# State-space scan: the 16 rotation tables made during the first projection tiles, kept in DRAM and loaded step by step

## The chip, the core and the metric
One core of a Trainium2 chip runs the whole kernel in one launch. The metric is the device time of that launch in microseconds (us); lower is better.

## The reference, cut to what matters
The kernel computes one block of a network on 512 tokens of width 2048: an RMS norm, a wide input projection, a state-space branch, an mLSTM branch, a gated merge, and a layer of experts. The change touches the state-space branch only.

```
proj = hn @ w_in          # split into u_ssm (512), xm (1536), z (1536), i, f, g_a (2048), g_b (2048)
a_bar  = exp(lam * dt)                                   # one complex number for each of 2048 states
bu     = einsum('gph,bsgh->bsgp', b_bar, u)              # complex input of every state, 512 tokens
states = scan over tokens: s[t] = a_bar * s[t-1] + bu[t]
y      = real(einsum('ghp,bsgp->bsgh', c, states)) + d_skip * u ; y = gelu(y)
```

The 2048 states are 16 blocks of 128 partitions. With a_bar = r * exp(i*theta), the kernel turns bu[t] back by the angle theta*t, runs two real scans with the factor r, and turns the result forward again. For this each block of states needs a table of cos(theta*t) and sin(theta*t), 128 x 512 each. That is a rotation table. The sixteen tables depend on the parameters alone, not on the tokens.

## The kernel before
**Engines and order.** The order on every engine is written out by hand, with semaphores. PE is TensorE, DVE is VectorE, ACT is ScalarE, POOL is GpSimd. SP issues the weight stream: one unit is a 128 x 2048 tile of weights (1024 KB) that lands in `raw[k]`, k = 0 or 1.

**One unit of the stream.** Products are made in fp32 as three matmuls of split operands. ACT copies `raw` to `whi` (line 653, in `split_hi`), DVE makes `wlo = raw - whi` (line 1038, in `split_lo`, called by `next_lo`), and PE does 48 matmuls of 512 columns (`proj`, lines 1732 to 1734). `split_hi` of unit u+1 waits until PE is done with unit u-1, since that frees `whi[k]` (the condition in `next_hi`, line 657). ACT then stores PE's result to DRAM (`spilled`, lines 688 to 695). So each unit passes ACT, DVE and PE in this order, and PE starts unit u+1 once `lo_done` has counted its `wlo`.

**The first projections.** Units 4 to 15 give xm and units 16 to 27 give z. DVE's part is two loops of `next_lo`: lines 1204 to 1206 (it makes `wlo` of units 5 to 16) and lines 1214 to 1216 (units 17 to 26). Between the two loops stand three small instructions on the gates (lines 1211 to 1213). The third counts `ge_sem` to 1, and ACT waits for that with an exponential (lines 701 and 702) that stands ahead of its `split_hi` of unit 17. Behind the second loop stands the gate section of DVE (lines 1218 to 1235). Its last instruction counts `ge_sem` to 3, and ACT waits for that at line 707, ahead of its `split_hi` of unit 27. DVE then makes `wlo` of units 27 and 28 (lines 1236 and 1237).

**The scan.** Units 28 to 59 (the gates g_a, g_b) share their stretch with the scan: 4 chunks c of 4 steps k (lines 1240 to 1291 on DVE, 1789 to 1806 on PE, 375 to 408 on POOL, 713 to 729 on ACT). A step of PE is: projection unit, the output matmuls of the step before (`s5_out`, lines 1784 and 1786), the two input products into `sc` (line 1804), a second projection unit. At the end of a chunk PE does `s5_out` of step 3 at once, so it waits for that step's `rout`. A step of DVE is: `wlo`; the rotation table of this block (lines 1249 to 1263: two memsets, then nine levels that each double the table with four instructions, 38 instructions in all); the rotation of the inputs (1267 to 1269), once ACT has copied `sc` to `bus` (line 723); two scans (1274, 1276); `wlo` of the next unit; the rotation back into `rout` (1280 to 1283). POOL does half of each rotation (lines 391 to 405). In a level, the second and the fourth instruction start without a wait; the others wait for the one before them.

**Addresses.** The cosines and sines of theta*2^lv of all 16 blocks are in `ptab`. POOL copies the four blocks of a chunk into the small tile `pc` (lines 382 and 383), and the level loop takes its two scalars as `pc[:, 0, lv, k:k + 1]` and `pc[:, 1, lv, k:k + 1]` (line 1253), whose addresses are constants. The only other place that matters here is the short convolution `conv` (lines 1294 to 1307): its scalars `tap` are addressed by `3 * h + c`. Called at line 1312, h is the constant 0; called from `head` (lines 1395, 1398 and 1404) inside the loop over heads, h is a loop register. 

`tab` has two buffers, so the table of step k may be written once the outputs of step k-2 are done.

Of the kernel before, what the change touches and what calls it, by code (L numbers as in the profile page):

```python
# [13 lines left out]
ALU = mybir.AluOpType  # L14
ACT = mybir.ActivationFunctionType
AX_X = mybir.AxisListType.X
F32 = mybir.dt.float32
# [4 lines left out]
P = 128  # L22
T = 512
# [3 lines left out]
SC, MC, HC = SSM_W // P, ML_W // P, HD // P  # L27
# [7 lines left out]
U_SSM, U_XM, U_Z, U_GA, U_GB = 0, 4, 16, 28, 44  # L35
# [28 lines left out]
HALF_PI = (1.5703125, 4.837512969970703125e-4, 7.54978995489188216e-8)  # L64
NEG_BIG = -3.0e38

S5_STEPS, ML_STEPS, PK_STEPS, PICK_STEPS = 164, 23, 67, 64


def build(nc, a, out_d):  # L70

    ctx = ExitStack()
    with ctx:
# [3 lines left out]
        def S(name, shape, dt, kb):  # L77

            size = 4 * int(np.prod(shape[1:]))
            assert kb * 1024 + size <= room, (name, kb * 1024 + size, room)  # L80
            return nc.alloc_sbuf_tensor_at(name, shape, dt, offset=base + int(kb * 1024))

        def sem(name):
            return ctx.enter_context(nc.semaphore(name))
# [28 lines left out]
        wif = S("wif", [P, KC, 64], F32, 164)  # L113
        bc = S("bc", [P, 2, P], F32, 168)
        cc = S("cc", [P, 2, 4, 32], F32, 169)
        pc = S("pc", [P, 2, 9, 4], F32, 170)
        rc = S("rc", [P, 8], F32, 170.5)
        cw = S("cw", [P, 40, 16], F32, 171)
        ptab = S("ptab", [P, 2, 9, 16], F32, 174)
        gt = S("gt", [P, 4, T], F32, 184)  # L120
        gout = S("gout", [P, 3, T], F32, 192)
        tab = S("tab", [P, 2, 2, T], F32, 112)
# [4 lines left out]
        dtmp = S("dtmp", [P, 2, T], F32, 136)  # L127
# [99 lines left out]


        spill = nc.dram_tensor("spill", (56, P, T), F32).ap()
        ya_d = nc.dram_tensor("ya_d", (KC, P, T), F32).ap()  # L230
        ev_d = nc.dram_tensor("ev_d", (NKEY * NKEY, D), F32).ap()
        gates_d = nc.dram_tensor("gates_d", (3, HEADS, T), F32).ap()
# [47 lines left out]
        idx_done, el_in, ac_done, acc_done = sem("idx_done"), sem("el_in"), sem("ac_done"), sem("acc_done")  # L280
        gv_in = [sem(f"gv_in{i}") for i in range(3)]
        acct_done, acct_free = sem("acct_done"), sem("acct_free")
        gn_in, upn_in = sem("gn_in"), [sem("upn_in0"), sem("upn_in1")]
        ev_out = sem("ev_out")
        fin_done, fin_out = sem("fin_done"), sem("fin_out")
# [52 lines left out]
        def _(pool):  # L338
            n = [0]
# [26 lines left out]
                                   ALU.subtract).then_inc(alo_done[1], 1)  # L366


            pool.wait_ge(gates_done, 1)
            pool.dma_start(gates_d.rearrange("g h t -> h g t"), gout[0:HEADS, :, :]).then_inc(gates_out, 16)  # L370


            pool.wait_ge(coef_done, 1)
            pool.wait_ge(proj_free, SC)
            with pool.Fori(0, SC) as c:

                pool.wait_ge(cm_done, 4 * c)
                pool.wait_ge(ylo_done, c)
                pool.tensor_copy(uc[:], uT[:, c, :])
                for r in range(2):  # L380
                    pool.tensor_copy(cc[:, r, :, :], cp[:, r, :, :].rearrange("p (c k) h -> p c k h", c=4)[:, c, :, :])
                    pool.tensor_copy(pc[:, r, :, :],
                                     ptab[:, r, :, :].rearrange("p n (c k) -> p c n k", c=4)[:, c, :, :])
                pool.tensor_copy(rc[:, 0:4], cw[:, 0, :].rearrange("p (c k) -> p c k", c=4)[:, c, :])
                pool.tensor_copy(rc[:, 4:5], vec[:, V_DSKIP:V_DSKIP + SC].rearrange("p (c k) -> p c k", k=1)[:, c, :])\
                    .then_inc(chunk_done, 1)
                for k in range(4):

                    pool.wait_ge(bus_done, 8 * c + 2 * k + 2)
                    pool.wait_ge(tab_done, 4 * c + k + 1)  # L390
                    pool.tensor_tensor(ptmp[:, 0, :], bus[:, 1, :], tab[:, k % 2, 0, :], ALU.mult).then_inc(pool_step, 1)
                    pool.tensor_tensor(ptmp[:, 1, :], bus[:, 0, :], tab[:, k % 2, 1, :], ALU.mult).then_inc(pool_step, 1)
                    pool.wait_ge(pool_step, 2 + 16 * c + 4 * k + 2)

                    pool.wait_ge(scan_done, 8 * c + 2 * k)
                    pool.tensor_tensor(rin[:, 1, :], ptmp[:, 0, :], ptmp[:, 1, :], ALU.subtract).then_inc(prot_done, 1)

                    pool.wait_ge(prot_done, 4 * c + k + 1)
                    pool.wait_ge(scan_done, 8 * c + 2 * k + 2)
                    pool.tensor_tensor(ptmp[:, 0, :], wst[:, 0, :], tab[:, k % 2, 1, :], ALU.mult).then_inc(pool_step, 1)  # L400
                    pool.tensor_tensor(ptmp[:, 1, :], wst[:, 1, :], tab[:, k % 2, 0, :], ALU.mult).then_inc(pool_step, 1)
                    pool.wait_ge(pool_step, 2 + 16 * c + 4 * k + 4)

                    pool.wait_ge(cm_done, 4 * c + k)
                    pool.tensor_tensor(rout[:, 1, :], ptmp[:, 0, :], ptmp[:, 1, :], ALU.add).then_inc(out_i_done, 1)

                pool.wait_ge(bu_done, 8 * c + 8)
                pool.dma_start(bc[:], a["b_tab"][c + 1]).then_inc(bc_in, 16)
# [598 lines left out]
        def _(dve):  # L1007
# [33 lines left out]
            def next_lo(m, k):  # L1041
                nm, nk = (m, 1) if k == 0 else (m + 1, 0)
                split_lo(nm, nk)
# [157 lines left out]
            tt(cp[:, 1, :, :], w0, cp[:, 1, :, :], ALU.add)  # L1201
            dve.tensor_scalar(cp[:, 1, :, :], cp[:, 1, :, :], -1.0, None, ALU.mult).then_inc(coef_done, 1)

            with dve.Fori(U_XM // 2, U_Z // 2) as m:
                for k in range(2):
                    next_lo(m, k)


            gi, g1, g2, gf = (gt[0:HEADS, i, :] for i in range(4))
# [1 line left out]
            ts(gi, pv[0][0:HEADS, :], vec[0:HEADS, V_BI:V_BI + 1], None, ALU.add)  # L1211
            ts(gf, pv[0][32:32 + HEADS, :], vec[32:32 + HEADS, V_BF:V_BF + 1], None, ALU.add)
            dve.scalar_tensor_tensor(g1, gf, -1.0, gf, ALU.mult, ALU.max).then_inc(ge_sem, 1)
            with dve.Fori(U_Z // 2, U_GA // 2 - 1) as m:
                for k in range(2):
                    next_lo(m, k)

            dve.wait_ge(ge_sem, 2)
            ts(g1, g2, 2.0, None, ALU.add)
# [18 lines left out]


            with dve.Fori(0, SC) as c:  # L1240
                one, count = stepper(s5_step, S5_STEPS * c)
                dve.wait_ge(chunk_done, c + 1)
                for k in range(4):
                    m = U_GA // 2 + 4 * c + k
                    next_lo(m, 0)

                    dve.wait_ge(out_i_done, 4 * c + k - 1 if k else 4 * c)
                    tc_, ts_ = tab[:, k % 2, 0, :], tab[:, k % 2, 1, :]
                    one(dve.memset(tc_[:, 0:1], 1.0), wait=False)
                    one(dve.memset(ts_[:, 0:1], 0.0))  # L1250
                    for lv in range(9):
                        w = 1 << lv
                        pcos, psin = pc[:, 0, lv, k:k + 1], pc[:, 1, lv, k:k + 1]
                        one(dve.tensor_scalar(dtmp[:, 0, 0:w], ts_[:, 0:w], psin, None, ALU.mult), wait=False)
                        one(dve.tensor_scalar(dtmp[:, 1, 0:w], ts_[:, 0:w], pcos, None, ALU.mult))
                        one(dve.scalar_tensor_tensor(tc_[:, w:2 * w], tc_[:, 0:w], pcos, dtmp[:, 0, 0:w],
                                                     ALU.mult, ALU.subtract), wait=False)
                        ins = dve.scalar_tensor_tensor(ts_[:, w:2 * w], tc_[:, 0:w], psin, dtmp[:, 1, 0:w],  # L1258
                                                       ALU.mult, ALU.add)
                        if lv < 8:  # L1260
                            one(ins)
                        else:
                            ins.then_inc(tab_done, 1)
                    dve.wait_ge(tab_done, 4 * c + k + 1)

                    dve.wait_ge(bus_done, 8 * c + 2 * k + 2)
                    one(dve.tensor_tensor(dtmp[:, 0, :], bus[:, 0, :], tc_, ALU.mult), wait=False)
                    one(dve.tensor_tensor(dtmp[:, 1, :], bus[:, 1, :], ts_, ALU.mult))
# [884 lines left out]
```

## Time and profile before

| what | value |
|---|---|
| time, median of 3 runs | 4286.54 us (4284.75 to 4287.95) |
| time of the profiled execution | 4285.1 us |
| its span, first to last instruction | 4283.6 us |
| PE busy | 4065.0 us (95%) |
| DVE busy | 2508.7 us (59%) |
| ACT busy | 1226.7 us (29%) |
| POOL busy | 1129.3 us (26%) |
| mean granted clock of PE | 0.973 of full speed |

The span is the profiled execution without what lies around it, here 1.5 us. Busy times count only instructions that work on data; matmuls overlap and their ends are modelled. In a timeline a row gives the start and the time of an instruction, and in brackets how long the engine had been idle before it and what released it. A row marked DVEq is work of DVE's sequencer (register arithmetic), not of its data path. A window row gives the busy time and the number of instructions of each engine, then the granted clock of PE (1.00 is 2.4 GHz, 0.5 is 1.2 GHz), the DMA share and the rate.

### The profile page before, as it was taken

To read this page: it belongs to the slowest core of one execution; us is meant where nothing else is said; L and a number is where in the kernel's file an instruction comes from. 1 tells how busy PE (TensorE), PEld (TensorE's weight loads), DVE (VectorE), ACT (ScalarE), POOL (GpSimd) and SP (SyncE) were. 2 spreads that over 40 slices of the span, in tenths; PEclk is the share of its full clock that TensorE was granted. 3 is DMA by queue.
4 is the path that set the end of the run, shared out by engine and by line. 5 is a ranking of instruction groups with operands and counts; after the bars stand their busy time and mean duration, and the time that the engine had idled before them with its cause. 6 is when DMAs were issued, how large, how long until landed. Compare 5 with 4: busy or idle time off the path is not lost.

```text
span 4283.6 us, 54780 instructions
## 1 busy us (share of the span) xinstructions
PE 4065.0 (95%) x19189; PEld 3474.4 (81%) x19189; DVE 2508.7 (59%) x3563; ACT 1226.7 (29%) x1282; POOL 1129.3 (26%) x742
## 2 busy tenths in 40 slices
PE   7999999887789989999999999999989999999997
PEld 4887666665677768888888888888879999999996
DVE  5226888837653254454566666222237888788874
ACT  3232222234322222222233333222222222232222
POOL 1002334433211144545300000000012444444432
PEclk9999999998899989999999999999999999999998
DMA  3332222342154344554677777866767888888883
GB/s 120 120 115 98 98 100 96 108 152 79 51 175 142 127 135 162 173 170 161 209 238 239 255 241 238 295 216 215 222 232 262 302 306 325 308 327 304 307 315 114
DMA packets 225639, 840.57 MB, mean 196 GB/s; under 512 B 21720, under 2 KB 60136, under 8 KB 157600
## 3 DMA queue, kind: packets, MB, share of 16 engines
q1 hardware_dynamic: 96432, 454.07, 29.3%
q10 hardware_dynamic: 95808, 207.64, 15.6%
q0 software_dynamic: 33328, 178.08, 11.5%
q8 instruction: 25, 0.41, 0.0%
q14 instruction: 46, 0.38, 0.0%
HBM read 753.70 MB, written 220.23 MB: 227 GB/s over the span
## 4 chain that ended last, share of the span: by engine, by line
PE 72%; DVE 13%; issue 6%; DMA 4%; ACT 3%; POOL 2%; DVEq 1%; ACTq 0%; SPq 0%; POOLq 0%
PE mm L1732 18%; PE mm L1733 18%; PE mm L1734 17%; DMA raw<-stream 3%; PE pv L1732 3%; PE pv L1733 3%; PE pv L1734 3%; DVE wlo L1038 2%; PE sc L1734 1%; PE sc L1733 1%; PE sc L1732 1%; DVE acc L1658 1%; ACT whi L653 1%; DVE tab L1258 1%; POOL el L611 1%
## 5 line engine op out<-in xcount | busy, mean ns | idle before, releaser
L1038 DVE TENSOR_TENSOR wlo<-raw,whi 128x2048 fp32r<-128x2048 f32 x328 | 753.4, 2297 | 882.4 <-ACT whi L653 881.9
L653 ACT ACTIVATE whi<-raw 128x2048 fp32r<-128x2048 f32 x380 | 727.4, 1914 | 499.6 <-issue 198.7
L1732 PE MATMUL mm<-t_hi,whi 128*128 128x512 f32 x2048 | 798.5, 390 | 0.0
L1733 PE MATMUL mm<-t_lo,whi 128*128 128x512 f32 x2048 | 797.8, 390 | 0.0
L1734 PE MATMUL mm<-t_hi,wlo 128*128 128x512 f32 x2048 | 797.3, 389 | 0.0
L1734 PEld LDWEIGHTS mm<-t_hi,wlo 128*128 128x128 f32 x2048 | 384.6, 188 | 80.4
L1732 PEld LDWEIGHTS mm<-t_hi,whi 128*128 128x128 f32 x2048 | 384.8, 188 | 78.1
L1733 PEld LDWEIGHTS mm<-t_lo,whi 128*128 128x128 f32 x2048 | 384.8, 188 | 77.7
L1732 PE MATMUL mm<-hn_hi,whi 128*128 128x512 f32 x960 | 380.6, 396 | 34.3 <-DVE hn_lo L1074 19.3
L1733 PE MATMUL mm<-hn_lo,whi 128*128 128x512 f32 x960 | 376.6, 392 | 0.0
L1734 PE MATMUL mm<-hn_hi,wlo 128*128 128x512 f32 x960 | 375.9, 392 | 0.0
L617 POOL DMA_INDIRECT gv<-ev_d,idx_v x128 | 230.1, 1798 | 513.7 <-DVE acc L1658 468.7
L550 POOL TENSOR_TENSOR wlo<-raw,whi 128x2048 fp32r<-128x2048 f32 x52 | 239.3, 4603 | 301.0 <-ACT whi L653 301.0
L1658 DVE SCALAR_TENSOR_TENSOR acc<-gv,ac,acc 128x2048 f32<-128x2048 f32 x127 | 298.2, 2348 | 32.5 <-DMA gv<-ev_d,idx_v 30.3
L894 ACT ACTIVATE sgl<-mm 128x512 f32<-128x512 f32 x128 | 76.7, 599 | 744.9 <-PE mm L1734 744.8
L1732 PEld LDWEIGHTS mm<-hn_hi,whi 128*128 128x128 f32 x960 | 181.7, 189 | 95.6 <-issue 33.8
L611 POOL DMA_INDIRECT el<-up_d,idx_e x128 | 198.2, 1548 | 88.0 <-DVE ac L1664 49.2
L1734 PEld LDWEIGHTS mm<-hn_hi,wlo 128*128 128x128 f32 x960 | 181.9, 189 | 38.5
L1733 PEld LDWEIGHTS mm<-hn_lo,whi 128*128 128x128 f32 x960 | 182.0, 190 | 36.5
L961 ACT ACTIVATE actb<-gl 128x384 f32 (+1 forms) x128 | 67.3, 526 | 492.5 <-DVE gl L1633 484.6
L1732 PE MATMUL pv<-actb,whi 128*128 (+1 forms) x512 | 173.0, 338 | 13.7 <-DVE wlo L1038 13.7
L1732 PE MATMUL mm<-actb,whi 128*128 (+1 forms) x512 | 171.7, 335 | 0.4 <-DVE wlo L1038 0.3
(395 smaller groups left out, 7553.1 us busy)
## 6 DMA issues: line engine op xcount, KB each, us to landing
raw<-stream SPq DMA_DIRECT2D x380, 1024.0 KB, 4.9
ev_d<-stream ACTq DMA_DIRECT2D x128, 1024.0 KB, 6.1
up_d<-sgl ACTq DMA_DIRECT2D x128, 256.0 KB, 2.1
g_d<-gst ACTq DMA_DIRECT2D x12, 2048.0 KB, 11.5
gg<-g_d SPq DMA_DIRECT2D x15, 1536.0 KB, 12.0
gl<-up_d SPq DMA_DIRECT2D x120, 192.0 KB, 5.0
spill<-stage ACTq DMA_DIRECT2D x56, 256.0 KB, 2.0
x<-xT SPq DMA_DIRECT2D x4, 1024.0 KB, 9.4
```

What stands on the lines that cost most here:

```text
L550: pool.tensor_tensor(wlo[:, nk, :], raw[:, nk, :], whi[:, nk, :].bitcast(F32), ALU.subtract)\
L611: pool.indirect_dma_start(el[:, s:s + 1], None, ups_flat, bass.IndirectOffsetOnAxis(ap=idx_e[:, s:s + 1], axis=0)).then_inc(el_in, 16)
L617: pool.indirect_dma_start(gv[s % 3][:], None, ev_d, bass.IndirectOffsetOnAxis(ap=idx_v[:, 0, s:s + 1], axis=0))\
L653: act.activation(whi[:, k, :], raw[:, k, :], ACT.Copy).then_inc(hi_done, 1)
L894: act.activation(sgl[:, k, :], mm[k][:], ACT.Gelu_apprx_tanh).then_inc(proj_free, 1)
L961: act.activation(actb[:, par, 0, v, :], gl[:, v % 2, :], ACT.Copy).then_inc(acthi_done, 1)
L1038: dve.tensor_tensor(wlo[:, k, :], raw[:, k, :], whi[:, k, :].bitcast(F32), ALU.subtract)\
L1258: ins = dve.scalar_tensor_tensor(ts_[:, w:2 * w], tc_[:, 0:w], psin, dtmp[:, 1, 0:w], ALU.mult, ALU.add)
L1658: dve.scalar_tensor_tensor(acc[:], gv[b][:], ac_cols[:, s, :], acc[:], ALU.mult, ALU.add)\
L1732: pe.matmul(out, lh, rh, start=start, stop=False)
L1733: pe.matmul(out, lh, rl, start=False, stop=False)
L1734: return pe.matmul(out, ll, rh, start=False, stop=stop)
```

## The change
The table of a block is no longer made in its step of the scan. DVE makes all sixteen during the projections: in the first loop one table behind every two units (6 tables), in the second loop one behind every unit (10 tables). POOL stores each table in a DRAM tensor `tab_d` when `tab_done` has counted it, and DVE waits for the store of two tables before it overwrites a buffer. In the scan POOL loads the table of a step, 512 KB, one step ahead (`table`), and DVE and POOL wait for the load (`tab_in`) where they waited for the table. The copies into `pc` are gone; the level loop takes its scalars from `ptab` at the place n, which is an expression of the loop register.

```
+        tab_d = nc.dram_tensor("tab_d", (4 * SC, P, 2, T), F32).ap()
@@ POOL
+            with pool.Fori(0, 2 * SC) as q:
+                for b in range(2):
+                    pool.wait_ge(tab_done, 2 * q + b + 1)
+                    pool.dma_start(tab_d[2 * q + b], tab[:, b, :, :]).then_inc(tab_out[b], 16)
             pool.wait_ge(gates_done, 1)
...
+            def table(n, k, half):
+                pool.wait_ge(tab_out[k % 2], 16 * 2 * SC)
+                pool.wait_ge(out_r_done, n - 1 if k else n)
+                pool.wait_ge(out_i_done, n - 1 if k else n)
+                pool.dma_start(tab[:, k % 2, :, :], tab_d[n]).then_inc(tab_in[k % 2], 16)
             with pool.Fori(0, SC) as c:
+                table(4 * c, 0, 2 * c)
...
-                    pool.tensor_copy(pc[:, r, :, :],
-                                     ptab[:, r, :, :].rearrange("p n (c k) -> p c n k", c=4)[:, c, :, :])
...
                 for k in range(4):
+                    if k < 3:
+                        table(4 * c + k + 1, k + 1, 0)
                     pool.wait_ge(bus_done, 8 * c + 2 * k + 2)
-                    pool.wait_ge(tab_done, 4 * c + k + 1)
+                    pool.wait_ge(tab_in[k % 2], 32 * c + 16 * (k // 2) + 16)
@@ DVE
-            with dve.Fori(U_XM // 2, U_Z // 2) as m:
-                for k in range(2):
-                    next_lo(m, k)
+            def rotation_table(n, b, half):
+                one, count = stepper(s5_step, TAB_STEPS * n)
+                dve.wait_ge(tab_out[b], 16 * half)
+                tc_, ts_ = tab[:, b, 0, :], tab[:, b, 1, :]
+                one(dve.memset(tc_[:, 0:1], 1.0), wait=False)
+                one(dve.memset(ts_[:, 0:1], 0.0))
+                for lv in range(9):
+                    w = 1 << lv
+                    pcos, psin = (ptab[:, r, lv, :].rearrange("p (q o) -> p q o", o=1)[:, n, :] for r in range(2))
+                    one(dve.tensor_scalar(dtmp[:, 0, 0:w], ts_[:, 0:w], psin, None, ALU.mult), wait=False)
+                    one(dve.tensor_scalar(dtmp[:, 1, 0:w], ts_[:, 0:w], pcos, None, ALU.mult))
+                    one(dve.scalar_tensor_tensor(tc_[:, w:2 * w], tc_[:, 0:w], pcos, dtmp[:, 0, 0:w],
+                                                 ALU.mult, ALU.subtract), wait=False)
+                    ins = dve.scalar_tensor_tensor(ts_[:, w:2 * w], tc_[:, 0:w], psin, dtmp[:, 1, 0:w],
+                                                   ALU.mult, ALU.add)
+                    if lv < 8:
+                        one(ins)
+                    else:
+                        ins.then_inc(tab_done, 1)
+            with dve.Fori(0, MC // 4) as j:
+                for b in range(2):
+                    for k in range(2):
+                        next_lo(U_XM // 2 + 2 * j + b, k)
+                    rotation_table(2 * j + b, b, j)
...
-            with dve.Fori(U_Z // 2, U_GA // 2 - 1) as m:
-                for k in range(2):
-                    next_lo(m, k)
+            with dve.Fori(0, U_GA // 2 - 1 - U_Z // 2) as j:
+                for k in range(2):
+                    next_lo(U_Z // 2 + j, k)
+                    rotation_table(MC // 2 + 2 * j + k, k, MC // 4 + j)
...
             with dve.Fori(0, SC) as c:
                 for k in range(4):
                     next_lo(m, 0)
-                    dve.wait_ge(out_i_done, 4 * c + k - 1 if k else 4 * c)
...
-                        pcos, psin = pc[:, 0, lv, k:k + 1], pc[:, 1, lv, k:k + 1]
...
-                    dve.wait_ge(tab_done, 4 * c + k + 1)
+                    dve.wait_ge(tab_in[k % 2], 32 * c + 16 * (k // 2) + 16)
                     dve.wait_ge(bus_done, 8 * c + 2 * k + 2)
```

## Rows read from the trace of the kernel before

**Rows 1.** Busy time by window, one of the z projections and one middle step of the scan
```profile
205.00:333.00 128.00, 128.00 (x566) 106.04 (x565) 29.59 (x15) 41.35 (x33) 0.00 (x0) 1.00 0.33 118
...
412.00:438.00 26.00, 26.00 (x106) 18.95 (x105) 24.71 (x50) 6.40 (x7) 11.14 (x6) 1.00 0.31 102
```

**Rows 2.** Timeline of PE: the input products of two steps that follow each other
```profile
413.33 1.98 PE L1804 MATMUL sc<-uc,bc 32*128 32x512 f32 x4
...
439.08 1.98 PE L1804 MATMUL sc<-uc,bc 32*128 32x512 f32 x4
```

**Rows 3.** Waits of PE in the scan (366 to 825 us): total us, times, longest us
```profile
PE dn L1784 <- DVE rout L1283: 18.3, 4, 4.7
PE mm L1732 <- DVE wlo L1038: 6.9, 4, 2.5
```

**Rows 4.** Timeline of DVE: the end of the xm projections, z projections, gate section
```profile
228.29 2.29 DVE L1038 TENSOR_TENSOR wlo<-raw,whi 128x2048 fp32r<-128x2048 f32 x1 [8.45 <-ACT whi L653]
230.50 1.51 DVE L1099 TENSOR_SCALAR gt<-pv,vec 4x512 f32<-4x512 f32 x2
...
240.94 2.29 DVE L1038 TENSOR_TENSOR wlo<-raw,whi 128x2048 fp32r<-128x2048 f32 x1 [8.22 <-ACT whi L653]
...
338.29 2.29 DVE L1038 TENSOR_TENSOR wlo<-raw,whi 128x2048 fp32r<-128x2048 f32 x1 [8.43 <-ACT whi L653]
340.50 0.41 DVE L1099 TENSOR_SCALAR gt<-gt 4x512 f32<-4x512 f32 x1
...
359.89 2.29 DVE L1038 TENSOR_TENSOR wlo<-raw,whi 128x2048 fp32r<-128x2048 f32 x1 [2.49 <-ACT whi L653]
```

**Rows 5.** Timeline of PE: the first matmul of unit 27
```profile
362.23 0.79 PE L1732 MATMUL mm<-hn_hi,whi 128*128 128x512 f32 x1 [6.82 <-DVE wlo L1038]
```

**Rows 6.** Timeline of DVE: the rotation table of step 1, chunk 0
```profile
407.53 0.06 DVE L1249 MEMSET tab<- 128x1 f32 x1
...
407.66 0.21 DVE L1254 TENSOR_SCALAR dtmp<-tab,pc 128x1 f32<-128x1 f32 x1
407.79 0.20 DVE L1255 TENSOR_SCALAR dtmp<-tab,pc 128x1 f32<-128x1 f32 x1
...
415.67 0.48 DVE L1258 SCALAR_TENSOR_TENSOR tab<-tab,pc,dtmp 128x256 f32<-128x256 f32 x1
```

**Rows 7.** Convolution on DVE: constant address, then a loop register; last the register instructions
```profile
831.76 0.54 DVE L1300 TENSOR_SCALAR cv<-xmr,vec 128x512 f32<-128x512 f32 x1
832.34 1.54 DVE L1302 SCALAR_TENSOR_TENSOR cv<-xmr,vec,cv 128x511 f32<-128x511 f32 x2
...
1002.36 0.75 DVE L1302 SCALAR_TENSOR_TENSOR cv<-xmr,vec,cv 128x511 f32<-128x511 f32 x1 [0.15 <-DVE cv L1300]
...
L1302 DVEq FUSED_REGOPS  x18: 57/57/65, 988.4 to 1065.6; - x18
```

**Rows 8.** Timeline of ACT: the exponential between the xm and the z projections
```profile
237.05 0.63 ACT L702 ACTIVATE gt<-gt 4x512 f32<-4x512 f32 x1 [0.68 <-ACT stage L693]
```

**Rows 9.** Timelines of ACT and DVE: `bus` and the rotation behind it, two steps
```profile
466.49 1.09 ACT L723 ACTIVATE bus<-sc 128x512 f32<-128x512 f32 x2 [2.74 <-PE sc L1804]
...
467.80 1.80 DVE L1267 TENSOR_TENSOR dtmp<-bus,tab 128x512 f32<-128x512 f32 x1
...
612.04 1.09 ACT L723 ACTIVATE bus<-sc 128x512 f32<-128x512 f32 x2 [0.70 <-ACT stage L693]
...
614.96 1.78 DVE L1267 TENSOR_TENSOR dtmp<-bus,tab 128x512 f32<-128x512 f32 x1
```

**Rows 10.** Timeline of DVE: the first rotation product in step 1 of chunk 2
```profile
642.00 0.69 DVE L1267 TENSOR_TENSOR dtmp<-bus,tab 128x512 f32<-128x512 f32 x1 [1.47 <-ACT bus L723]
```

**Rows 11.** Timeline of PE behind its longest wait for `wlo`; busy time by window
```profile
624.83 0.64 PE L1732 MATMUL mm<-hn_hi,whi 128*128 128x512 f32 x1 [2.46 <-DVE wlo L1038]
...
625.00:635.50 10.50, 10.50 (x40) 8.53 (x41) 10.11 (x24) 0.53 (x1) 4.13 (x3) 0.84 0.52 169
```

**Rows 12.** DMA issues on POOL's queue: KB each, median us to landing
```profile
sz<-spill POOLq DMA_DIRECT2D x4, 768.0 KB, 7.0
```

More of the change, by code:

```diff
@@ L65 @@
 NEG_BIG = -3.0e38
-S5_STEPS, ML_STEPS, PK_STEPS, PICK_STEPS = 164, 23, 67, 64
+S5_STEPS, TAB_STEPS, ML_STEPS, PK_STEPS, PICK_STEPS = 16, 37, 23, 67, 64
 def build(nc, a, out_d):
@@ L115, in build @@
         cc = S("cc", [P, 2, 4, 32], F32, 169)
-        pc = S("pc", [P, 2, 9, 4], F32, 170)
         rc = S("rc", [P, 8], F32, 170.5)
@@ L282, in build @@
         acct_done, acct_free = sem("acct_done"), sem("acct_free")
+        tab_out, tab_in = [sem("tab_out0"), sem("tab_out1")], [sem("tab_in0"), sem("tab_in1")]
         gn_in, upn_in = sem("gn_in"), [sem("upn_in0"), sem("upn_in1")]
@@ L1202, in _ @@
             dve.tensor_scalar(cp[:, 1, :, :], cp[:, 1, :, :], -1.0, None, ALU.mult).then_inc(coef_done, 1)
-            with dve.Fori(U_XM // 2, U_Z // 2) as m:
-                for k in range(2):
-                    next_lo(m, k)
+            def rotation_table(n, b, half):
[17 more added lines that the diff above has]
+                        ins.then_inc(tab_done, 1)
+                assert count[0] == TAB_STEPS, count
+            with dve.Fori(0, MC // 4) as j:
[3 more added lines that the diff above has]
+                    rotation_table(2 * j + b, b, j)
             gi, g1, g2, gf = (gt[0:HEADS, i, :] for i in range(4))
@@ L1240, in _ @@
             with dve.Fori(0, SC) as c:
-                one, count = stepper(s5_step, S5_STEPS * c)
+                one, count = stepper(s5_step, TAB_STEPS * 4 * SC + S5_STEPS * c)
                 dve.wait_ge(chunk_done, c + 1)
@@ L1245, in _ @@
                     next_lo(m, 0)
-                    dve.wait_ge(out_i_done, 4 * c + k - 1 if k else 4 * c)
                     tc_, ts_ = tab[:, k % 2, 0, :], tab[:, k % 2, 1, :]
[L1249 to L1252, printed above, removed]
-                        pcos, psin = pc[:, 0, lv, k:k + 1], pc[:, 1, lv, k:k + 1]
[L1254 to L1263, printed above, removed]
-                    dve.wait_ge(tab_done, 4 * c + k + 1)
+                    dve.wait_ge(tab_in[k % 2], 32 * c + 16 * (k // 2) + 16)
                     dve.wait_ge(bus_done, 8 * c + 2 * k + 2)
```

## The prediction
> **What bounds the kernel now.** I first read the busy time by window. In the z projections PE is busy for all of the 128 us, with 566 matmuls, 0.226 us each, so a unit of 48 takes 10.86 us; DVE works 29.59 us of the 128 [rows 1]. There PE is the bound and DVE has room. In a middle step of the scan both are full: PE 26.00 of 26 us, DVE 24.71 [rows 1]. The question is which of the two sets the step. The timeline of PE answers it: from one pair of input products to the next it is 25.75 us [rows 2], and the list of PE's waits has only eight entries in the whole scan [rows 3]: four for `rout` at the chunk ends (18.3 us together) and four for `wlo` (6.9 us), one in step 0 of each chunk. The twelve other steps have no wait of PE. So in the scan PE is the bound too, DVE is the bound for 25.2 us in all, and that is the most that freeing DVE can return, apart from the clock.
>
> The place to look at next is where the work goes. The timeline of DVE shows the ten `wlo` of the z projections (first and last shown), then the gate section from 340.50 us on, and `wlo` of unit 27 at 359.89 [rows 4]. PE stood idle for 6.82 us before that unit [rows 5]. So the chain DVE gate section, ACT, DVE `wlo`, PE is already late there: whatever delays the start of the gate section delays PE one for one, however idle DVE was on the way.
>
> **What leaves the scan.** A table takes from 407.53 to 415.67 + 0.48 = 416.15, that is 8.62 us [rows 6]; 16 of them are 138 us of DVE. Most of that lies under PE's units. The gain is how much earlier the rotation starts. It needs the table and `bus`; where the table is in time, DVE waits for `bus` alone [rows 10]. In step 0 of chunk 2 `bus` is done at 613.13 and the rotation starts at 614.96, 1.8 us late [rows 9]; the same step is 0.8, 0.7 and 0.9 us late in the other chunks. The `wlo` behind it comes earlier by that, 4.1 us for the four. The wait of 2.46 us in chunk 2 is also followed by a stretch at 0.84 granted clock, a part of it at the lower level, 1.2 GHz [rows 11]; with 0.8 us of wait left, as long as the waits that stayed at full clock or shorter, I count 0.16 x 10.5 = 1.7 us back. In step 3 the rotation starts 0.2 us late [rows 9], up to 0.3 in the other chunks: 1 us for the four chunk ends. A rotation that starts with DVE ahead of POOL has a first product of 0.69 us where it otherwise takes 1.8 [rows 9, 10]; I count a few tenths for that. The sum is **7 us gained**, with 3 and 12 as the ends. The copies into `pc` are off every path, since the `wlo` behind them waits for ACT: nothing.
>
> **What comes to the projections: the tables.** Their instructions are the same, but the scalars are now addressed by a loop register. The convolution has both forms. With constant addresses the next instruction starts 0.04 us behind the end of the last (831.76 + 0.54, then 832.34); with a loop register it is 0.15, and DVE's sequencer shows one register instruction of 57 ns for each [rows 7]. A table has 18 instructions that wait for the one before, so it grows by 18 x 0.11 = 2.0 us. The other 18 follow at 0.13 us (407.66 to 407.79 us in the smallest level) and no row shows a register instruction inside such a pair: bounds are nothing, if it fits into the 0.13, and 57 ns each, 1.0 us. I take the middle: the table is 8.6 + 2.0 + 0.5 = **11.1 us**, ends 10.6 and 11.6. A `wlo` ahead of it takes 2.21 us until the next instruction starts (228.29 to 230.50) [rows 4]. In the second loop DVE then needs 13.3 us a unit against PE's 10.86.
>
> The Trainium skill speaks against this term: "VectorE: DVE Perf Modes", section "The DRAIN you can't avoid", says that the next instruction starts only when the pipe is empty and that a semaphore between two costs nothing extra. If register work hid in the same way the table would stay at 8.6 us. The convolution's 0.15 against 0.04 us is the measurement, and it decides for my sum.
>
> **What comes to the projections: the path.** In the first loop a table stands behind every two units, 2 x 2.21 + 11.1 = 15.5 us of 21.7: it fits. The `wlo` behind a table finds 8.45 us of idle time [rows 4] filled with 11.1, so it is 2.7 us late. PE has more in hand: `wlo` of unit 16 was ready at 230.58 [rows 4] and PE came to it at about 235.8 (ACT's copy of PE's result, 0.6 us, and 0.68 idle lie ahead of the exponential at 237.05 [rows 8]). The sixth table starts at 230.50, where the gate instructions start now; those took until 240.94 - 8.22 = 232.72, 2.22 us [rows 4]. They now end at 230.50 + 11.1 + 2.22 = 243.8. ACT's exponential waits for them and started at 237.05 [rows 8]; `wlo` of unit 17 came 3.89 us behind it (240.94) [rows 4, 8]. Now it comes at 243.8 + 3.9 = 247.7. From there DVE does ten times `wlo` and table, without a pause since it is the slower one: 247.7 + 10 x 13.31 = 380.8 is the new start of the gate section, against 340.50 [rows 4]. In general it is 258.7 + 11 x table. So the chain is **40.3 us later**; with tables of 10.6 and 11.6 us, 34.8 and 45.8. Even with tables of 8.62 it is 13.0. All that follows, the gate section, ACT, `wlo`, unit 27 at 362.23 [rows 5], and the scan behind, moves by this. PE's waits between units are about 2.4 us each, near the 2.46 that was followed by the lower clock [rows 11]; units of 12.6 us still fit into 13.3, so that costs nothing more. PE's idle time before unit 27 becomes some 22 us; it restarts at 1.2 GHz in the kernel before too (first matmuls of 0.79 and 0.64 us behind both waits [rows 5, 11]), so I add nothing.
>
> **The DMAs and the new waits.** POOL issues a store behind each table. It has nothing else there, and DVE overwrites a buffer two tables later, 13 us at least. In the scan a load is issued when the step before has its outputs, about 8 us before the next `bus`. A load of 512 KB lies between nothing and the 7.0 us of 768 KB on the same queue [rows 12]; I take it as hidden. Behind POOL's wait for `rout` is only its own next rotation, which needs the later `bus`. Cost nothing; if the cover were gone, up to 1 us a step.
>
> **Sum.** 4285.1 us (the profiled execution: span 4283.6 and 1.5 around it) + 40.3 - 7 = 4318.4. The median lies 1.4 above that execution, so I say **4320 us**.
>
> **Rivals.**
> - *Register work is hidden.* The table stays at 8.6 us. For it: in the scan each wait of the table has a threshold that is computed in a register, and the table of 8.62 us [rows 6] holds all of them. Against: the convolution's rows [rows 7]. Then 13.0 - 7 = 6: 4293 us. Chance 0.09. It is also what the skill's rule above would give.
> - *Register work costs more.* Each of the 36 instructions pays 0.11 us, since a register instruction breaks the pair too: table 12.6 us, chain 57 us later, 4336 us. Nothing shows it, but no row excludes it. Chance 0.13.
> - *Faster.* DVE sets PE's waits in the scan, as its 24.71 of 26 us suggest [rows 1], and with the tables gone all 25.2 us of waits [rows 3] and 1.7 of clock go. It decides only if the tables cost no register time: 13.0 - 26.9 = -13.9, 4273 us. Against: a chunk end's wait comes from the rotations and scans themselves, which take a unit of 10.86 and up to 4.7 of wait [rows 1, 3], with the table or without. Chance 0.03.
> - *The work doesn't leave the path.* Loads arrive late and each step waits as it did for a table: the gain of 7 is gone, 4327 us. Chance 0.03.
>
> **How the numbers follow.** The forecast, tables of 10.6 to 11.6 us and a gain of 3 to 12, has 0.72 and its own range is 4309 to 4330; its rarer ends and a register cost of two thirds give 4304. About 0.2% (8.6 us) is what a measurement of this kernel can tell from no change. The range of 8 in 10 is 4304 to 4336: it leaves out the hidden register work, the faster case and half of the dearer case. Slower by over 0.2% is the forecast, the dearer tables and the late loads, 0.88 (to 4295 us counts as the same); the first rival lies just inside, 0.09; faster 0.03.
>
> **What would show it.** In the changed kernel: the first instructions of the table pairs with 0.15 us ahead of them and one register instruction of 57 ns for each pointer; a table of some 11 us; ten `wlo` in the z projections with no idle time of DVE ahead of them, 13.3 us apart; `wlo` of unit 17 near 247.8 us; the gate section starting near 381; PE idle some 22 us before unit 27; in the scan, waits of PE for `wlo` of 0 to 1 us and unchanged steps of 25.75. It would be wrong if the gate section starts before 370 (tables cheaper), or if PE's waits at the chunk ends shrink by more than 1 us each.

## The result and the profile after

The changed kernel takes 4301.47 us, the median of 8 runs (4299.31 to 4305.13), against 4285.61 us for the kernel before (8 runs): 15.9 us more, ratio 1.0037, 95% interval 1.0027 to 1.0047. I had forecast 4320 us, with a range from 4304. The direction was right and the time lies outside the range.

| | before | after | forecast |
|---|---|---|---|
| profiled execution, span, us | 4283.6 | 4301.1 | |
| one table, us | 8.62 (in the scan) | 9.64 | 11.1 |
| gate section starts at, us | 340.50 | 364.88 | 380.8 |
| PE starts unit 27 at, us | 362.23 | 387.23 | about 402.5 |
| last matmul of the last chunk, `dn`, starts at, us | 822.36 | 839.84 | |
| gain in the scan, us | | 7.5 | 7 |

Down the last two rows: unit 27 is 25.0 us late, the last `dn` matmul is 17.5 us late, so the scan gave back 7.5 us, and the span is 17.5 us longer. So behind the scan nothing was gained or lost.

**A table.** The timeline of DVE in the xm projections: the table behind `wlo` of unit 16, its memset, first two levels, last instruction, and what follows it.

```profile
230.21 0.06 DVE L1224 MEMSET tab<- 128x1 f32 x1
...
230.46 0.21 DVE L1229 TENSOR_SCALAR dtmp<-tab,ptab 128x1 f32<-128x1 f32 x1 [0.18 <-DVE tab L1225]
230.59 0.21 DVE L1230 TENSOR_SCALAR dtmp<-tab,ptab 128x1 f32<-128x1 f32 x1
230.84 0.22 DVE L1231 SCALAR_TENSOR_TENSOR tab<-tab,ptab,dtmp 128x1 f32<-128x1 f32 x1
230.97 0.21 DVE L1233 SCALAR_TENSOR_TENSOR tab<-tab,ptab,dtmp 128x1 f32<-128x1 f32 x1
231.33 0.23 DVE L1229 TENSOR_SCALAR dtmp<-tab,ptab 128x2 f32<-128x2 f32 x1
...
239.37 0.48 DVE L1233 SCALAR_TENSOR_TENSOR tab<-tab,ptab,dtmp 128x256 f32<-128x256 f32 x1
239.76 1.51 DVE L1114 TENSOR_SCALAR gt<-pv,vec 4x512 f32<-4x512 f32 x2
```

The view of a single line also counts the instructions of DVE's sequencer (DVEq). The first and the second line of a level have one of them each time; the third, L1231, has none, and its row shows DVE alone. The same holds for the fourth, L1233.

```profile
L1229 DVEq FUSED_REGOPS  x144: 57/57/64, 121.9 to 363.3; - x144
...
L1230 DVEq FUSED_REGOPS  x144: 53/57/57, 122.0 to 363.5; - x144
...
L1231 DVE SCALAR_TENSOR_TENSOR tab<-tab,ptab,dtmp x144: 218/235/486, 122.4 to 364.1; 128x1 f32<-128x1 f32 x16, 128x2 f32<-128x2 f32 x16, 128x4 f32<-128x4 f32 x16, 128x8 f32<-128x8 f32 x16
```

Read the gaps. Before the first instruction of a level it is 0.15 us (230.97 + 0.21 = 231.18, then 231.33), as the convolution had shown [rows 7]. Before the third it is 0.04 (230.59 + 0.21, then 230.84), the gap of a constant address. L1229 makes the register for `psin`, L1230 the one for `pcos`, and L1231 and L1233 use those again. The register instruction of L1230 has no price either: L1230 starts 0.13 us behind L1229, just as in the kernel before [rows 6]. So 9 of the 18 waiting instructions pay 0.11 us, not 18, and the in-pair ones nothing: 8.62 + 9 x 0.11 = 9.6, and 9.64 was measured (230.21 to 239.85, the end of L1233).

**The chain.** The timeline of DVE again, its `wlo` of units 17, 18, 25 and 26, the start of the gate section, and `wlo` of unit 27.

```profile
245.92 2.29 DVE L1053 TENSOR_TENSOR wlo<-raw,whi 128x2048 fp32r<-128x2048 f32 x1 [3.93 <-ACT whi L668]
...
257.99 2.28 DVE L1053 TENSOR_TENSOR wlo<-raw,whi 128x2048 fp32r<-128x2048 f32 x1
...
341.19 2.29 DVE L1053 TENSOR_TENSOR wlo<-raw,whi 128x2048 fp32r<-128x2048 f32 x1
...
352.99 2.28 DVE L1053 TENSOR_TENSOR wlo<-raw,whi 128x2048 fp32r<-128x2048 f32 x1
...
364.88 0.41 DVE L1114 TENSOR_SCALAR gt<-gt 4x512 f32<-4x512 f32 x1
...
384.27 2.91 DVE L1053 TENSOR_TENSOR wlo<-raw,whi 128x2048 fp32r<-128x2048 f32 x1 [2.49 <-ACT whi L668]
```

From unit 18 to unit 26 no `wlo` has idle time ahead of it, where each had 8.2 to 8.4 us [rows 4]. They stand 11.9 us apart against the 10.86 of a unit on PE. The prediction's formula, 258.7 + 11 x table, gives 364.7 for the measured table; the gate section starts at 364.88, 24.4 us late. Unit 27 is 25.0 us late on PE, 0.6 more, since its `wlo` takes 2.91 us where it took 2.29 [rows 4]. It takes 2.9 us in the six kernels in which POOL issues a load of a table just ahead of its copy into `uc` (after, e1, e2, e4, e6 and e7), so that this copy of 0.62 us falls inside `wlo`, and 2.29 in the four in which it doesn't (before, e3, e3b and e5). No run tried whether the copy is the cause. PE pays for the delay at unit 27, with the same half-speed start as before [rows 5] but three times the idle time. The longer wait has no clear price of its own in clock: over the 11 us behind this start the granted clock is 0.85 before and 0.78 after, but 0.72 in e4 with 7.4 us of idle time and 0.85 in e5 with 20.

```profile
387.23 0.80 PE L1755 MATMUL mm<-hn_hi,whi 128*128 128x512 f32 x1 [20.64 <-DVE wlo L1053]
```

**The scan.** The waits of PE from 385 to 850 us, in the columns of [rows 3].

```profile
PE mm L1755 <- DVE wlo L1053: 22.9, 5, 20.6
PE dn L1807 <- DVE rout L1306: 17.2, 4, 4.3
```

Of the 22.9 us, 20.6 are the one before unit 27; the other four, in the first steps, are 2.3 us together, where they were 6.9. The chunk ends wait 17.2 us instead of 18.3. That is 4.6 + 1.1 = 5.7 us of the 7.5. The wait in chunk 2 is now short enough that the clock stays up behind it: 1.00 in the window below, against 0.84 [rows 11], the 1.7 us that the forecast had. Elsewhere in the scan the clock falls a little more than before, by 0.7 us, if windows of 11 us are summed from unit 27 on (12.0 us lost to the clock before, 11.0 after). So some 0.8 us of the 7.5 are not accounted for. By window (columns: PE, PE weight load, DVE, ACT and POOL busy, granted clock, DMA share, GB/s):

```profile
645.00:656.00 11.00, 10.44 (x46) 8.50 (x46) 7.89 (x5) 2.52 (x2) 5.69 (x4) 1.00 0.62 192
```

Two middle steps in the same columns, and behind them the input products that mark a step on PE:

```profile
438.00:464.00 26.00, 26.00 (x106) 19.13 (x106) 16.81 (x10) 6.12 (x6) 12.19 (x7) 1.00 0.36 128
464.00:490.00 26.00, 26.00 (x105) 19.09 (x106) 16.84 (x10) 6.12 (x6) 11.55 (x6) 1.00 0.32 105
```

```profile
438.11 1.98 PE L1827 MATMUL sc<-uc,bc 32*128 32x512 f32 x4
...
463.83 1.55 PE L1827 MATMUL sc<-uc,bc 32*128 32x512 f32 x3
```

DVE works 16.8 us of 26 instead of 24.71 [rows 1], a third less, and a step takes 463.83 - 438.11 = 25.72 us instead of 25.75 [rows 2]. PE was the bound of the scan, as read. The DMA issues say that the new transfers are far from late: a load lands 3.6 us behind its issue (median), and each of the 16 first rotation products waits for `bus`, none for a table.

```profile
tab<-tab_d POOLq DMA_DIRECT2D x16, 512.0 KB, 3.6
...
415.41 0.69 DVE L1290 TENSOR_TENSOR dtmp<-bus,tab 128x512 f32<-128x512 f32 x1 [7.89 <-ACT bus L738]
```

### The profile page after: what moved, and what is told of

The parts are those of the page before. It is cut to its first block, busy times and chain, and to the rows that moved or that the text cites. A ratio compares the mean times of both kernels' runs of the same rounds, so it can differ in the third digit from the quotient of the medians.

```text
span 4301.1 us, 55215 instructions
## 1 busy us (share of the span) xinstructions
PE 4066.4 (95%) x19189; PEld 3473.8 (81%) x19189; DVE 2507.5 (58%) x3563; ACT 1226.9 (29%) x1282; POOL 1148.0 (27%) x766
## 4 chain that ended last, share of the span: by engine, by line
PE 79%; DVE 10%; issue 4%; DMA 2%; ACT 2%; POOL 2%; DVEq 1%; ACTq 0%; SPq 0%; POOLq 0%
PE mm L1755 19%; PE mm L1756 19%; PE mm L1757 18%; PE pv L1755 3%; PE pv L1757 3%; PE pv L1756 3%; DVE wlo L1053 2%; DMA raw<-stream 2%; PE sc L1756 2%; PE sc L1757 2%; PE sc L1755 2%; ACT whi L668 1%; PE st L1757 1%; PE dn L1756 1%; PE st L1756 1%
## 5 line engine op out<-in xcount | busy, mean ns | idle before, releaser
L1755 PE MATMUL pv<-actb,whi 128*128 (+1 forms) x512 | 173.3, 339 | 14.8 <-DVE wlo L1053 14.7
L1756 PE MATMUL pv<-actb,whi 128*128 (+1 forms) x512 | 172.2, 336 | 0.0
```

The lines of the kernel that those rows point to most:

```text
L1755: pe.matmul(out, lh, rh, start=start, stop=False)
L1756: pe.matmul(out, lh, rl, start=False, stop=False)
```

## The experiments

**Theory**: the time is set by the start of the gate section, that is by 11 tables in a row on DVE, of 9.64 us each because 9 waiting instructions a table make a register pointer; the scan gains 7.5 us, nearly all in the first steps. **Rivals**: the register pointers cost nothing and the tables are long for another reason; the time comes from the amount of work, stores or loads wherever they stand; the scan gains or loses something that the projections hide. The kernels were run in two sets, each with its own runs of the kernel before: 4282.81 us (21 runs) for the first four, 4282.55 us (27 runs) for the others. Against those, the ratio of 1.0037 puts the changed kernel at 4298.7 and at 4298.4 us.

**e1_constant: the register pointers taken away.** Both loops of DVE are written out, so that every pointer is a constant.

```
-            with dve.Fori(0, MC // 4) as j:
+            for j in range(MC // 4):
...
-            with dve.Fori(0, U_GA // 2 - 1 - U_Z // 2) as j:
+            for j in range(U_GA // 2 - 1 - U_Z // 2):
```

> The two projection loops of DVE are unrolled, so the scalars of the tables have constant addresses; nothing else differs from the changed kernel. Chain theory (the table's own length counts eleven times, gate section at 258.7 + 11 x table): the table falls from 9.64 us to 8.6, the gate section starts at about 353 us instead of 364.9, and the time is 4301.5 - 11 = 4290 us. Rival (the loss comes from the stores and loads, or from the amount of DVE work, not from addressing): table and time stay, 4301 us. Rival 2 (unrolled code costs DVE instruction fetching): table 9 us or more with gaps inside, 4295 to 4301 us.

Measured: 4289.07 us (11 runs), ratio 1.0012 [1.0003, 1.0021]. The last `wlo` of the z projections, the first big gate instruction (L1260, at 365.32 us in the changed kernel), and the start of a table:

```profile
231.51 0.21 DVE L1229 TENSOR_SCALAR dtmp<-tab,ptab 128x1 f32<-128x1 f32 x1
231.65 0.21 DVE L1230 TENSOR_SCALAR dtmp<-tab,ptab 128x1 f32<-128x1 f32 x1
...
343.13 2.28 DVE L1053 TENSOR_TENSOR wlo<-raw,whi 128x2048 fp32r<-128x2048 f32 x1
...
354.34 3.34 DVE L1260 RECIPROCAL gt<-gt 4x512 f32<-4x512 f32 x1
```

The gate section is 10.98 us earlier than in the changed kernel, 1.0 us for each of 11 tables, and the step inside the pair is 0.14 us with a constant and 0.13 with a register. So the pointers cost 1.0 us a table and none of it in the pair. A table takes 8.63 us here, which leaves nothing for the other rival of this run, that written-out code is slower. The kernel is still slower than before: tables of 8.6 us leave a chain that is late, as the prediction's 13.0 us for this case said.

**e2_pointer_each: a register pointer for every instruction.** A second copy of the angle table, read by the third and fourth instruction of each level, so that L1231's pointers can't be those of L1229 and L1230.

```
+                    pcos_b, psin_b = (ptab_b[:, r, lv, :].rearrange("p (q o) -> p q o", o=1)[:, n, :] for r in range(2))
...
-                    one(dve.scalar_tensor_tensor(tc_[:, w:2 * w], tc_[:, 0:w], pcos, dtmp[:, 0, 0:w],
+                    one(dve.scalar_tensor_tensor(tc_[:, w:2 * w], tc_[:, 0:w], pcos_b, dtmp[:, 0, 0:w],
```

> The third and fourth instruction of each level read a second copy of the angle table at another address, so they need a register instruction of their own: nine more waits with a register instruction behind them for each table, which is what my prediction had assumed. Theory: each costs some 0.09 to 0.11 us, the table is 10.5 us, the gate section starts near 374 us and the time is 4301.5 + 9 to 11 = 4311 us. Rival (register work hides and the 0.11 us has another cause, such as the loop or the tile): 4301 us.

Measured: 4307.93 us (5 runs), ratio 1.0054 [1.0040, 1.0068], 9.3 us above the changed kernel on the same scale.

```profile
231.59 0.21 DVE L1233 TENSOR_SCALAR dtmp<-tab,ptab 128x1 f32<-128x1 f32 x1
231.93 0.22 DVE L1234 SCALAR_TENSOR_TENSOR tab<-tab,ptab_b,dtmp 128x1 f32<-128x1 f32 x1
...
374.97 3.34 DVE L1263 RECIPROCAL gt<-gt 4x512 f32<-4x512 f32 x1
```

```profile
L1234 DVEq ALU_OP  x144: 40/40/40, 123.4 to 373.6; - x144
```

The third instruction now has 0.13 us ahead of it instead of 0.04. Its register instruction is another one, ALU_OP of 40 ns and not FUSED_REGOPS of 57, and it costs 0.09 us where the other costs 0.11. A table takes 10.44 us here (231.22 to 241.66), 0.80 more, which is 9 x 0.09. The gate section is 9.65 us later, 0.88 us a table. That is close to the lower end of the prediction, 10.6 us: all 18 waits pay and the pairs nothing. With e1 this brackets the changed kernel from both sides: the price is in the waiting instructions that make a pointer, and their count is what I had wrong.

**e5_proj_alone: the half in the projections.** All 16 tables are made and stored there, as in the changed kernel; the scan is that of the kernel before and makes its own tables again, with no loads, once all stores are done. Against the kernel before, besides the function `rotation_table`, its two calls and the stores:

```
-                    pool.wait_ge(tab_done, 4 * c + k + 1)
+                    pool.wait_ge(tab_done, 16 + 4 * c + k + 1)
...
-                one, count = stepper(s5_step, S5_STEPS * c)
+                one, count = stepper(s5_step, TAB_STEPS * 4 * SC + S5_STEPS * c)
```

> The projections are those of the changed kernel, with all sixteen tables made and stored, and the scan is that of the kernel before, which makes each table again and loads none. Theory: the gate section starts 24.4 us late and the scan gains nothing: 4285.6 + 24.5 = 4310 us. Rival (part of the delay is made good later, since work that waits in the scan is shifted too): 4300 to 4306 us.

**e4_scan_alone: the half in the scan.** Two tables are made early, with constant addresses, and stored eight times each; the scan loads as in the changed kernel. It leaves out the 14 other tables. Against the changed kernel:

```
-                    rotation_table(2 * j + b, b, j)
+                    if j == 0:
+                        rotation_table(b, b, 0)
...
-                    next_lo(U_Z // 2 + j, k)
-                    rotation_table(MC // 2 + 2 * j + k, k, MC // 4 + j)
+                    next_lo(m, k)
```

> Only two tables are made, behind the first two pairs of xm units, and each is stored eight times; the z loop is that of the kernel before. The scan loads one table a step as the changed kernel does. Left out: the other fourteen tables. Theory: the gate section starts at 340.5 as before and the scan keeps its gain of 7.5 us: 4285.6 - 7.5 = 4278 us. Rival (the loads cost something in the scan that the gain hides, or the gain comes from another place): 4283 to 4286 us.

Measured: e5 4307.57 us (5 runs), 1.0059 [1.0045, 1.0072], that is 24.8 us slower; e4 4275.3 us (11 runs), 0.9984 [0.9975, 0.9993], 7.5 us faster. Together 17.3 us slower, and the change is 15.9: the two halves add up. The waits of PE from 300 to 850 us, of e5 and then of e4:

```profile
PE mm L1765 <- DVE wlo L1044: 27.8, 7, 20.1
PE dn L1817 <- DVE rout L1316: 18.3, 4, 4.7
```

```profile
PE dn L1807 <- DVE rout L1306: 17.2, 4, 4.3
PE mm L1755 <- DVE wlo L1053: 9.7, 5, 7.4
```

In e5 the chunk ends wait 18.3 us, as before; in e4 17.2 us, as after, and 7.4 of its 9.7 us are the old wait ahead of unit 27 (6.8 us before; the rest is the longer `wlo`). From the first matmul of unit 27 to the last `dn` matmul it is 460.1 us before, 452.6 after, 452.5 in e4 and 459.7 in e5: the gain in the scan is there with the loads and gone without them. e5 came out at 4307.57 us, between its theory (4310) and its rival (4306 at most); a part of the delay that is made good later is at most 0.4 us by this measure.

**e3_two_late: only the place of two tables.** Tables 14 and 15 are made behind the gate section, where DVE waited 14.37 us for `whi` before `wlo` of unit 29. **e3b_two_late_const** does the same with both loops written out.

```
-            with dve.Fori(0, U_GA // 2 - 1 - U_Z // 2) as j:
+            with dve.Fori(0, U_GA // 2 - 2 - U_Z // 2) as j:
...
+            for k in range(2):
+                next_lo(U_GA // 2 - 2, k)
...
             for k in range(2):
                 next_lo(U_GA // 2 - 1, k)
+            for k in range(2):
+                rotation_table(14 + k, k, 7)
```

> The changed kernel, but its last two tables (14 and 15) are made behind the gate section and the two wlo that follow it, where DVE was idle for 14.4 us before wlo of unit 29; the tables stay loop-addressed, their number, stores and loads are the same. Theory (only the start of the gate section counts): it starts some 15 us earlier, near 349.5 us instead of 364.9, and the kernel takes about 4286 us, 1.001 times the kernel before. Rival (the time is the amount of DVE work, stores or loads, wherever it stands): no change, 4301 us. If the two tables in their new place delay wlo of unit 29 past PE, some 5 us of the 15 are given back: 4291.

> As the kernel with two late tables, but with both loops written out, so that every pointer is a constant address and a table takes 8.57 us instead of 9.64. Theory: DVE keeps up with PE in the z projections, the gate section starts within 2 us of its old 340.5, and the gain of 7.5 us in the scan is all that is left: 4277 us, 0.9985. Rival (the gain in the scan is lost to something else once the tables are late, such as wlo of unit 29): 4283 or more.

Measured: e3 4285.85 us (11 runs), 1.0009 [1.0000, 1.0019]; e3b 4277.22 us (11 runs), 0.9986 [0.9977, 0.9995]. The work and the transfers are the same, and the loss of 15.9 us is down to 3.3 in the one (at the edge of what can be told from none) and a gain of 5.3 in the other. So the amount of work is not what costs. The timeline of DVE in e3, with `wlo` of units 26, 27 and 29:

```profile
348.79 2.29 DVE L1056 TENSOR_TENSOR wlo<-raw,whi 128x2048 fp32r<-128x2048 f32 x1 [4.06 <-ACT whi L671]
351.44 3.34 DVE L1265 RECIPROCAL gt<-gt 4x512 f32<-4x512 f32 x1
...
370.38 2.29 DVE L1056 TENSOR_TENSOR wlo<-raw,whi 128x2048 fp32r<-128x2048 f32 x1 [2.49 <-ACT whi L671]
...
397.49 2.29 DVE L1056 TENSOR_TENSOR wlo<-raw,whi 128x2048 fp32r<-128x2048 f32 x1 [3.34 <-POOL rc L401]
```

The gate section is 13.9 us earlier than after, and in e3b it starts at 341.6, 1.1 us behind the kernel before. A new wait shows, too: the last two stores sit on POOL's queue ahead of its copies for the first chunk, and DVE waits 3.34 us for `rc`. PE feels little of it:

```profile
PE sc L1834 <- POOL rc L401: 0.7, 1, 0.7
```

**e6_first_steps_only: the part of the scan that pays.** The kernel before, but the four tables of the first steps are made in the first four xm pairs, stored, and loaded; the twelve others stay in the scan.

```
+            for j in range(MC // 2):
                 for k in range(2):
-                    next_lo(m, k)
+                    next_lo(U_XM // 2 + j, k)
+                if j < 4:
+                    rotation_table(j, j % 2, j // 2)
```

> The kernel before, but only the four tables of the first steps of the chunks are made in the projections, in the first four xm pairs with constant addresses, where DVE is idle for 8.4 us and more and nothing on the chain to the gate section moves; they are stored and loaded, the twelve others are made in the scan as before. Theory (the tables of the middle steps lay wholly under PE, only those of the first steps were late): nearly all of the gain stays, 5.5 to 6.5 of the 7.5 us, and the gate section starts at 340.5 as before: 4277 us, 0.9986. Rival (the gain of 7.5 us comes from DVE having less to do in all steps, a quarter of it here): 4281 us, 0.9996.

Measured: 4277.52 us (11 runs), ratio 0.9986 [0.9977, 0.9995], 5.0 us faster by the medians and 6 by the ratio. With four tables it has what e3b has with sixteen. The rival's 0.9996 lies just outside the interval; the trace speaks more clearly, with 453.9 us from unit 27 to the last `dn` against 460.1 before, 6.2 us gained by four tables where sixteen gain 7.5. The waits show what is missing from e4's 7.5 us: the chunk ends stay at 18.7 us, since the last steps still make their tables.

```profile
PE dn L1827 <- DVE rout L1326: 18.7, 4, 4.7
PE mm L1775 <- DVE wlo L1052: 9.7, 5, 7.4
```

**e7_gates_spread: the late link itself.** On top of e6, the gate section is cut into three pieces, behind `wlo` of units 18, 19 and 20.

```
+            for k in range(2):
+                next_lo(U_Z // 2, k)
             dve.wait_ge(ge_sem, 2)
             ts(g1, g2, 2.0, None, ALU.add)
...
+            next_lo(U_Z // 2 + 1, 0)
             for d in (15, 13, 11, 9, 7, 5, 3):
...
+            next_lo(U_Z // 2 + 1, 1)
             one_b = ones[0:HEADS, 0:1].to_broadcast([HEADS, T])
...
+            with dve.Fori(U_Z // 2 + 2, U_GA // 2 - 1) as m:
+                for k in range(2):
+                    next_lo(m, k)
```

> As the kernel with the four first tables alone, and besides the gate section of DVE (16.9 us in one piece) is cut into three pieces behind wlo of units 18, 19 and 20, each shorter than the 8.4 us of idle time there. Theory (the gate section is the late link of the chain DVE, ACT, DVE, PE, already in the kernel before): PE's wait before unit 27, 6.8 us, goes nearly whole, with 1 to 2 us of lower clock behind it: 4269 us, 0.9967. Rival (PE's wait there has another end, such as ACT's table load or whi): the wait stays above 3 us and the time within 2 us of 4277.

Measured: 4268.58 us (5 runs), ratio 0.9964 [0.9950, 0.9978]: 14.0 us faster than the kernel before, 8.9 faster than e6, and the best of all. The waits of PE from 300 to 850 us:

```profile
PE dn L1831 <- DVE rout L1330: 18.7, 4, 4.7
...
PE mm L1779 <- DVE wlo L1052: 2.2, 4, 0.6
```

The wait of 7.4 us ahead of unit 27 is gone whole. So is the lower clock behind it. By window, the 11 us that begin with unit 27 in e6 (363.81 us), and in e7 two windows that follow each other and hold the same unit:

```profile
363.80:374.80 11.00, 10.99 (x41) 8.96 (x42) 2.29 (x1) 1.34 (x1) 0.90 (x6) 0.83 0.60 209
```

```profile
350.00:361.00 11.00, 11.00 (x50) 9.13 (x49) 4.79 (x2) 3.98 (x4) 4.04 (x8) 1.00 0.48 168
361.00:372.00 11.00, 11.00 (x51) 9.09 (x50) 0.95 (x2) 3.80 (x3) 0.00 (x0) 1.00 0.31 119
```

The granted clock is 0.83 of full in the first, a part of it at the level of 1.2 GHz, and 1.00 in the others: 0.17 x 11 = 1.9 us more. 7.4 + 1.9 = 9.3, and 8.9 was measured, by the medians and in the traces, where the last `dn` matmul starts at 808.82 us against 817.70 in e6. (The whole profiled execution of e7, 4273.66 us, is the longest of its five and only 1.6 us shorter than that of e6; the difference arises behind the scan.)

## Why the prediction was right, and where it was wrong

**What bounds the kernel: right.** PE bounds both stages. Freeing 138 us of DVE in the scan moved no middle step, and the place that decides is the chain from the gate section to unit 27. e3, which moves two tables with their stores and nothing else, shows it.

**The gain in the scan: right.** Forecast 7 us, measured 7.5 in the trace and 7.5 in e4, with some 0.8 us of it not attributed. e6 confirms that most of it, 5 to 6 us, belongs to the four first steps. The largest terms came out as put: 4.6 us of waits for `wlo` (4.1 forecast), 1.1 at the chunk ends (1.0), the clock in chunk 2 (1.7).

**The table: wrong, and this is the step that failed.** It was the sentence "A table has 18 instructions that wait for the one before, so it grows by 18 x 0.11 = 2.0 us", with the 0.5 us for the pairs behind it. The price of 0.11 us was right. The count was not: a level has two scalars, and each gets its register once, at its first use, so only one of the two waiting instructions of a level pays. The diff shows it to whoever looks for it (`pcos` and `psin` are made once a level and used twice); I had counted uses. The pairs cost nothing, the lower end of my bounds. So the term is 1.0 us, not 2.5, and it stands in the sum 11 times: 11 x 1.46 = 16.1 us. With the measured table and nothing else changed, the prediction's own sum is 4285.1 + 24.2 - 7 = 4302.3 us; the profiled execution after took 4302.6 (span 4301.1 and 1.5 around it). The prediction had named the sign: it would be wrong if the gate section started before 370, and it starts at 364.88.

**The path: right.** "258.7 + 11 x table" held in three kernels, within 1.0 us. e1, with tables of 8.63 us (231.38 to 240.01): 353.6, measured 354.34 - 0.44 = 353.9. The changed kernel: 364.7 and 364.88. e2, with 10.44 us: 373.5 and 374.97 - 0.44 = 374.5. (The 0.44 is the short instruction ahead of the reciprocal.)

**The bounds.** My lower end of the range took two thirds of the register cost as its least. The true value, two fifths, fell into a hole between "all 18 wait" and "hidden" (4293 us), to which no case was given. A count that is not shown by any row deserves a case of its own, however sure the price of one is.

**The rule on hidden register work.** A pointer adds nothing at the second instruction of a pair (0.13 us from start to start), and 0.11 us at an instruction that waits. The Trainium skill ("VectorE: DVE Perf Modes", section "The DRAIN you can't avoid") says that the next instruction starts only when the pipe is empty and that a semaphore between two costs nothing extra. It says nothing of register work there; that this hides in the same way was my extension of it. The extension would have given 4293 us, and e1 shows it wrong. Of the semaphore itself the trace agrees only in part: an instruction that waits starts 0.04 us behind the end of the one before, but one without a wait starts 0.08 us ahead of that end (230.59, against 230.46 + 0.21 = 230.67).

**The other rivals.** *Costs more*: the pair is not broken by a register instruction, and e2, with twice the pointers, is still at 4308. *Faster*: the chunk ends gave 1.1 us of their 18.3. *Late loads*: the prediction had a load issued "about 8 us before the next `bus`". The code gives it more, since a load for step n is issued when step n - 2 has its outputs, and even that of a first step has 18.0 us:

```profile
618.12 0.54 POOL L385 DMA_DIRECT2D tab<-tab_d  x1 [0.66 <-DVE rout L1306]
...
636.14 1.70 POOL L406 TENSOR_TENSOR ptmp<-bus,tab 128x512 f32<-128x512 f32 x1 [9.84 <-ACT bus L738]
```

PE's idle time before unit 27 was 20.6 us where I had said some 22. The 0.6 us that `wlo` of unit 27 takes longer stood at nothing in the prediction.

**Not settled.** Between 257 and 365 us five levels of the changed kernel start 0.25 to 0.51 us behind the end of the one before, instead of 0.15. No run asked for the cause. The waits of DVE have them, 1.5 us in all (the other row is the step from the memsets to the first product, 0.18 us a table):

```profile
DVE dtmp L1229 <- DVE tab L1225: 1.6, 9, 0.2
DVE dtmp L1229 <- DVE tab L1233: 1.5, 5, 0.5
```

## What to carry to other kernels

Moving work off an engine into "idle" time is free only if nothing that is in order behind it on that engine is already late. Look first for the one wait of the bound engine in the stage that receives the work, and follow its chain back; here that was 6.8 us before unit 27, and the best change was to shorten that chain, with the four tables that mattered placed well ahead of it. When a loop register comes into an address, count the pointers that are made (first uses, in the body) rather than the instructions that read them, and only those at an instruction that waits for the one before.

## What the runs showed of the hardware that I had not expected

- A pointer made from a loop register costs nothing at an instruction that does not wait for its predecessor (0.13 us from start to start with a register, 0.14 with a constant), and 0.09 to 0.11 us at one that does. The lower figure goes with a register instruction of 40 ns (ALU_OP, in e2), the higher with one of 57 ns (FUSED_REGOPS).
- DVE's first rotation product takes 0.69 us where it starts ahead of POOL's (415.41 against 415.57 us in the changed kernel), and 1.8 us where it doesn't [rows 9]. The scan behind it then is the slower one, 2.20 us against 1.23. The kernel before has both forms: 1.80 and 1.23 us in one step (467.80 [rows 9] and 473.03), 0.69 and 2.19 in another (642.00 [rows 10] and 646.13). From the product's start to the end of that scan it is 6.46 us in the first and 6.32 in the second, and 6.34 after. So the start ahead of POOL is worth some 0.1 us a step, not the 1.1 us by which the product is shorter, and less than the "few tenths" that I had counted. In three steps the first product takes 1.4 us (at 416.63, 529.02 and 754.67), and there the stretch is 6.1 us, the shortest. The slower scan starts while POOL is still at its own subtraction (419.04 to 420.66 us after, against 419.55); in the kernel before that has ended, at 420.92, before the scan of 1.23 us starts at 421.50. Whether that is the reason was not tried.

The scan of the changed kernel:

```profile
419.55 2.20 DVE L1297 TENSOR_TENSOR_SCAN wst<-rc,rin 128x512 f32<-128x512 f32 x1
```

The scans of the two steps of the kernel before:

```profile
473.03 1.23 DVE L1274 TENSOR_TENSOR_SCAN wst<-rc,rin 128x512 f32<-128x512 f32 x1
...
646.13 2.19 DVE L1274 TENSOR_TENSOR_SCAN wst<-rc,rin 128x512 f32<-128x512 f32 x1
```
